# The first mixer's three output projections: from fp32 products to split products in the heads' three weight slots

## The reference, cut to what matters

```
y_a = o.reshape(b, s, V_W) @ w_gdn_proj              # o: the eight heads' outputs, normed and gated
y_b = (gb * causal_depthwise_conv(gc * xin, sc_conv_w)) @ w_sc_out
mix = (gate_a * y_a + gate_b * y_b) @ w_o
```

## Time and profile before

| what | value |
|---|---|
| median of 3 runs | 1449.14 us (1444.05, 1449.14, 1450.11) |
| profiled execution, its own time | 1441.25 us |
| its span, first to last instruction | 1439.5 us |
| mean granted TensorE clock | 0.977 |
| PE, DVE, ACT busy | 94%, 62%, 45% of the span |
| L742, all three projections | 256 + 128 records, busy 58.8 + 28.0 us |
| DMA | 188 GB/s mean |

### The profile page before, as it was taken

How to read it: one execution, slowest core, us unless ns; L and a number is a source line. 1 busy time by engine, 2 the same in 40 slices (tenths; PEclk the granted TensorE clock), 3 DMA queues, 4 the chain that set the end, 5 groups by cost and what they waited for, 6 DMA issues and landing times.

```text
span 1439.5 us, 26382 instructions
## 1 busy us (share of the span) xinstructions
PE 1355.4 (94%) x9801; PEld 1236.9 (86%) x9801; DVE 894.9 (62%) x1680; ACT 643.2 (45%) x1171; POOL 14.9 (1%) x82
## 2 busy tenths in 40 slices
PE   6999999999999899999799987999999999999997
PEld 3888889988888799999578876999996777899996
DVE  0677887877623477778555635787785432775553
ACT  2555554555331355444555424555443331544542
POOL 4000000000000000000000000000000000000000
PEclk9999999999999899999899999999999999899998
DMA  9655545655692189889568812898896272666562
GB/s 310 194 162 162 175 121 159 178 159 161 177 248 59 33 245 268 265 245 317 147 207 255 228 44 77 252 271 263 242 317 226 76 195 70 178 203 185 158 182 88
DMA packets 400018, 269.95 MB, mean 188 GB/s; under 512 B 9915, under 2 KB 357425, under 8 KB 399937
## 3 DMA queue, kind: packets, MB, share of 16 engines
q1 hardware_dynamic: 399936, 268.83, 63.4%
HBM read 267.75 MB, written 1.05 MB: 187 GB/s over the span
## 4 chain that ended last, share of the span: by engine, by line
PE 83%; DVE 8%; ACT 3%; issue 2%; SPq 2%; DMA 1%; DVEq 0%; ACTq 0%
PE bank L756 18%; PE bank L758 18%; PE bank L757 18%; PE bank L742 6%; PE bank L818 4%; PE bank L728 2%; DVE w_low L1828 2%; PE bank L1150 1%; PE bank L952 1%; PE bank L953 1%; PE bank L944 1%; PE bank L1179 1%; DVE h_parts L1844 1%; SPq L527 1%; ACT w_high L1343 1%
## 5 line engine op out<-in xcount | busy, mean ns | idle before, releaser
L756 PE MATMUL bank<-h_parts,w_high 128*128 128x256 f32 x1824 | 547.9, 300 | 18.2 <-DVE h_parts L1844 15.7
L757 PE MATMUL bank<-h_parts,w_high 128*128 128x256 f32 x1824 | 520.2, 285 | 0.0
L758 PE MATMUL bank<-h_parts,w_low 128*128 128x256 f32 x1824 | 520.0, 285 | 0.0
L1828 DVE TENSOR_TENSOR w_low<-w_raw,w_high 128x1024 fp32r<-128x1024 f32 (+2 forms) x324 | 361.6, 1124 | 100.1 <-ACT w_high L1343 88.6
L756 PEld LDWEIGHTS bank<-h_parts,w_high 128*128 128x128 f32 x1824 | 352.8, 193 | 40.2 <-issue 24.9
L757 PEld LDWEIGHTS bank<-h_parts,w_high 128*128 128x128 f32 x1824 | 354.4, 194 | 2.9 <-issue 2.6
L758 PEld LDWEIGHTS bank<-h_parts,w_low 128*128 128x128 f32 x1824 | 353.5, 194 | 0.0
L1343 ACT ACTIVATE w_high<-w_raw 128x1024 fp32r<-128x1024 f32 (+2 forms) x324 | 312.9, 973 | 64.9 <-DMA w_raw<-in_w_ffn_out 19.5
L756 PE MATMUL bank<-act_parts,w_high 128*128 128x256 f32 x528 | 148.7, 282 | 0.0
L1335 ACT ACTIVATE evac<-bank 128x256 f32<-128x256 f32 x140 | 53.6, 383 | 212.1 <-PE bank L758 188.1
L757 PE MATMUL bank<-act_parts,w_high 128*128 128x256 f32 x528 | 147.3, 279 | 0.0
(11 more groups left out here) (360 smaller groups left out, 1576.4 us busy)
## 6 DMA issues: line engine op xcount, KB each, us to landing
ada_w<-in_ada_w SPq DMA_DIRECT2D x48, 1024.0 KB, 6.2
w_raw<-in_ffn_w_in SPq DMA_DIRECT2D x88, 512.0 KB, 4.1
w_raw<-in_w_in SPq DMA_DIRECT2D x72, 512.0 KB, 3.9
w_raw<-in_w_ffn_in SPq DMA_DIRECT2D x44, 512.0 KB, 4.0
ada_w<-in_w_ada SPq DMA_DIRECT2D x16, 1024.0 KB, 7.6
w_raw<-in_gla_w_in SPq DMA_DIRECT2D x24, 512.0 KB, 6.1
w_raw<-in_ffn_w_out SPq DMA_DIRECT2D x32, 384.0 KB, 4.8
w_raw<-in_ffn_w_out SPq DMA_DIRECT2D x32, 320.0 KB, 3.4
```

What stands on the lines that cost most here:

```text
L756: pe.matmul(acc[:, 0:T], hi[:, n, :], x_parts[:, k, 0, :], start=k == 0, stop=False)
L757: pe.matmul(acc[:, 0:T], hi[:, n, :], x_parts[:, k, 1, :], start=False, stop=False)
L758: mm = pe.matmul(acc[:, 0:T], lo[:, n, :], x_parts[:, k, 0, :], start=False, stop=k == kb - 1)
L1828: dve.tensor_tensor(w_low[:, s, 0:m], w_raw[:, s, 0:m], w_high[:, s, 0:m].bitcast(F32), ALU.subtract)\
```

## The change

The three projections become split products of one stream `st_p` of 24 pieces, which follows the heads' 72 in the same three slots: `w_sc_out` 0 to 7, `w_gdn_proj` 8 to 15 (`PA`), `w_o` 16 to 23 (`O1`). Their operands get halves as well:
- `ybin` becomes `y_high` and `y_low`. In `short_conv` DVE's one multiply becomes three instructions: the product rounded, the product again in fp32, and the difference. This stands in every head.
- For `w_gdn_proj` the parts go to `h1_parts`: in the eighth recurrence one ACT copy of seven blocks (128 x 1792) for the high halves, two DVE subtractions (four and three blocks) for the low ones, and two small DVE instructions for the last block.
- For `w_o` each block of `hT` gets `mix_high` on ACT and `mix_low` on DVE, in `h_parts`.

DVE and ACT make the weights' halves at the places where the heads' are made. In the eighth recurrence these are `low1(2)` to `low1(8)` and pieces 9 and 10; afterwards piece j+3 follows block j.

```diff
...
     pieces = 0
+    last_piece = {}
...
         SplitStream.pieces += n * per
+        self.raw_free = [SplitStream.last_piece.get(s, 0) for s in range(slots)]
...
-        oall, ybin = big[:, 0:KB, :], big[:, KB:2 * KB, :]
+        oall = big[:, 0:KB, :]
+        y_high = h_parts[:, KB // 2:KB, :, :].rearrange("p k a t -> p (k a) t")
+        y_low = ring_rest[:, 0:KB * T].rearrange("p (k t) -> p k t", t=T)
...
         st_h1 = SplitStream(H1, 9, slots=3)
-        for at in H1_SLOTS:
-            Stream.slot_user[at] = st_h1.end
-        st_pb = Stream(1, KB, [3, 7, 11, 0, 1, 2, 4, 5])
-        st_pa = Stream(1, KB, [6, 8, 9, 10, 3, 0, 1, 2])
-        st_o1 = Stream(1, KB, [12, 13, 14, 15, 16, 17, 7, 11])
+        st_p = SplitStream(1, 3 * KB, slots=3)
+        PA, O1 = KB, 2 * KB
+        for at in range(SplitStream.RINGS, 2 * HALF):
+            Stream.slot_user[at] = st_p.end
...
                 for j in range(st.per):
-                    if j >= st.slots or follows:
+                    if st is st_f1 and j < st.slots:
+                        if st.raw_free[j]:
+                            sp.wait_ge(S("split"), st.raw_free[j])
+                    elif j >= st.slots or follows:
...
             wo = kview(a["w_o"][0])
-            load_all(st_pb, wb)
-            load_all(st_pa, wa, range(4))
-            load_all(st_o1, wo, range(6))
-            load_ada(A_FFN1)
-            load_all(st_pa, wa, range(4, KB))
-            load_all(st_o1, wo, range(6, KB))
+            def ada2(i, j):
+                if j == PA + 2:
+                    load_ada(A_FFN1)
+            split_stream(st_p, lambda i, j: (wb, wa, wo)[j // KB][:, :, j % KB * P:(j % KB + 1) * P], IN_PARTS, extra=ada2, follows=True)
...
+                x_high, x_low = x_parts if isinstance(x_parts, tuple) else (x_parts[:, :, 0, :], x_parts[:, :, 1, :])
...
                                           ready=None if chain or j else ("h_low", 0))
-                        elif j < st_pb.per:
-                            pe.wait_ge(S("short"), 5 * H1)
-                            block_product(st_pb, 0, j, bank[j % 3], ybin, 3, part=[k])
+                        elif j < KB:
+                            if k == 0:
+                                pe.wait_ge(S("short"), 7 * H1)
+                                pe.wait_ge(S("evacuated"), st_p.done(0, j) + 3 - 3)
+                            split_product(st_p, 0, j, bank[j % 3], (y_high, y_low), IN_PARTS[0], KB, part=[k])
...
             head1(H1, False, True)
-            pe.wait_ge(S("evacuated"), st_pa.block0 + 3)
+            pe.wait_ge(S("evacuated"), st_p.done(0, PA - 1) + 3)
+            pe.wait_ge(S("part_low"), 2)
             for j in range(2):
-                block_product(st_pa, 0, j, bank[j], oall, 2, part=range(H1 - 1))
+                split_product(st_p, 0, PA + j, bank[j], h1_parts, IN_PARTS[0], KB, part=range(H1 - 1))
             pe.wait_ge(S("mod_ready"), 3)
-            pe.wait_ge(S("head_out"), H1)
+            pe.wait_ge(S("part_low"), 3)
             for j in range(KB):
-                block_product(st_pa, 0, j, bank[j % 2], oall, 2, part=[H1 - 1] if j < 2 else None)
+                pe.wait_ge(S("evacuated"), st_p.done(0, PA + j) + 3 - 2)
+                split_product(st_p, 0, PA + j, bank[j % 2], h1_parts, IN_PARTS[0], KB, part=[H1 - 1] if j < 2 else None)
...
                     norm_sum(1, range(KB - 2))
-                block_product(st_o1, 0, j, bank[j % 2], hT, 2, ready=("mix_ready", 0))
+                pe.wait_ge(S("evacuated"), st_p.done(0, O1 + j) + 3 - 2)
+                split_product(st_p, 0, O1 + j, bank[j % 2], h_parts, IN_PARTS[0], KB, ready=("part_low", 3) if j == 0 else None)
...
                     high(st_h1, i + 1, j - 6, IN_PARTS)
+                else:
+                    high(st_p, 0, j - 6, IN_PARTS)
...
                             copy_out1(i, j, last)
-                        elif j < st_pb.per:
-                            copy_out(st_pb, 0, j, hT[:, j, :], 3)
+                        elif j < KB:
+                            copy_out(st_p, 0, j, hT[:, j, :], 3)
+                            high(st_p, 0, j + 3, IN_PARTS)
...
                     copies(4 + 2 * l)
+                    if not gemm and l == 2:
+                        act.wait_ge(S("gemm_done"), st_h1.end)
+                        act.wait_ge(S("head_out"), H1 - 1)
+                        act.activation(h1_parts[:, 0:H1 - 1, 0, :], oall[:, 0:H1 - 1, :], ACT.Copy).then_inc(S("part_high"), 1)
...
+            def mix_high(j):
+                act.wait_ge(S("mix_ready"), j + 1)
+                act.activation(h_parts[:, j, 0, :], hT[:, j, :], ACT.Copy).then_inc(S("part_high"), 1)
...
                 act.wait_ge(S("mixed"), j + 1)
-                copy_out(st_pa, 0, j, evac[:, j % 2, :], 2)
-            out_blocks(st_o1, "o_added", 0, 4, 2)
+                copy_out(st_p, 0, PA + j, evac[:, j % 2, :], 2)
+                if j:
+                    mix_high(j - 1)
+                high(st_p, 0, PA + j + 3, IN_PARTS)
+            mix_high(KB - 1)
+            for j in range(KB):
+                act.wait_ge(S("o_added"), j + 1)
+                copy_out(st_p, 0, O1 + j, evac[:, j % 4, :], 2, scale=mod[:, 2 * KB + j:2 * KB + j + 1])
+                if O1 + j + 3 < st_p.per:
+                    high(st_p, 0, O1 + j + 3, IN_PARTS)
...
-                dve.wait_ge(S("short"), 5 * n + TAPS2 + 1)
-                dve.tensor_tensor(part(ybin, i), scv, scb, ALU.mult).then_inc(S("short"), 1)
+                dve.wait_ge(S("short"), 7 * n + TAPS2 + 1)
+                dve.tensor_tensor(part(y_high, i), scv, scb, ALU.mult).then_inc(S("short"), 1)
+                dve.tensor_tensor(scv, scv, scb, ALU.mult).then_inc(S("short"), 1)
+                dve.wait_ge(S("short"), 7 * n + TAPS2 + 3)
+                dve.tensor_tensor(part(y_low, i), scv, part(y_high, i).bitcast(F32), ALU.subtract).then_inc(S("short"), 1)
...
+                def low1(j):
+                    if gemm:
+                        low(st_h1, i, j, IN_PARTS)
+                    else:
+                        low(st_p, 0, j, IN_PARTS)
...
                     dve.tensor_scalar(gmat[:, NT + t, :], ident[:, :], hcur[:, 2 + t:3 + t], None, ALU.mult).then_inc(S("gmat"), 1)
-                if gemm:
-                    low(st_h1, i, 2, IN_PARTS)
+                low1(2)
...
 ...
...
                         convolve(i, l - 1)
-                    if gemm:
-                        if l < LEVELS - 1:
-                            low(st_h1, i, l + 4, IN_PARTS)
-                        elif not last:
-                            low(st_h1, i + 1, 0, IN_PARTS)
+                    if l < LEVELS - 1:
+                        low1(l + 4)
+                    elif gemm and not last:
+                        low(st_h1, i + 1, 0, IN_PARTS)
+                    else:
+                        low(st_p, 0, 0 if gemm else 9, IN_PARTS)
+                    if not gemm and l in (3, 4):
+                        at = slice(0, 4) if l == 3 else slice(4, H1 - 1)
+                        dve.wait_ge(S("part_high"), 1)
+                        dve.tensor_tensor(h1_parts[:, at, 1, :], oall[:, at, :], h1_parts[:, at, 0, :].bitcast(F32), ALU.subtract)\
+                           .then_inc(S("part_low"), 1)
...
                     short_conv(i)
-                    if not last:
-                        low(st_h1, i + 1, 1, IN_PARTS)
+                if gemm and not last:
+                    low(st_h1, i + 1, 1, IN_PARTS)
+                else:
+                    low(st_p, 0, 1 if gemm else 10, IN_PARTS)
...
                 dve.wait_ge(S("silu"), 2 * n)
+                if not gemm:
+                    dve.tensor_tensor(h1_parts[:, c, 0, :], part(oall, c), onrm, ALU.mult).then_inc(S("part_high"), 1)
                 dve.tensor_tensor(part(oall, c), part(oall, c), onrm, ALU.mult).then_inc(S("head_out"), 1)
+                if not gemm:
+                    dve.wait_ge(S("part_high"), 2)
+                    dve.wait_ge(S("head_out"), H1)
+                    dve.tensor_tensor(h1_parts[:, c, 1, :], part(oall, c), h1_parts[:, c, 0, :].bitcast(F32), ALU.subtract)\
+                       .then_inc(S("part_low"), 1)
...
             dve.wait_ge(S("gates"), 2)
-            dve.wait_ge(S("evacuated"), st_pb.end + 3)
+            dve.wait_ge(S("evacuated"), st_p.done(0, PA - 1) + 3)
...
             dve.wait_ge(S("gated"), 1)
+            def mix_low(j):
+                dve.wait_ge(S("part_high"), 2 + j + 1)
+                dve.tensor_tensor(h_parts[:, j, 1, :], hT[:, j, :], h_parts[:, j, 0, :].bitcast(F32), ALU.subtract).then_inc(S("part_low"), 1)
             for j in range(KB):
-                dve.wait_ge(S("evacuated"), st_pa.done(0, j) + 3)
+                dve.wait_ge(S("evacuated"), st_p.done(0, PA + j) + 3)
...
                 dve.sem_inc(S("mixed"), 1)
+                if j:
+                    mix_low(j - 1)
```

(36 more changed lines are left out.)

22 lines of the change are left out of this document (9 added, 13 removed).

## The result

| | before | after |
|---|---|---|
| median of 9 runs each | 1449.14 us | 1439.28 us |
| lowest to highest | 1444.05 to 1451.58 | 1435.62 to 1444.85 |
| profiled execution, its own time and span | 1441.25, 1439.5 us | 1440.99, 1439.3 us |
| its mean granted clock | 0.977 | 0.971 |

The medians of these runs lie 9.9 us apart. Forecast were 8.1 less and 1441.0. Yet the two profiled executions have the same time. That of before, 1441.25 us, was faster than all 55 timed runs of that kernel here (1442.8 and more), at a clock near the top of the 0.966 to 0.978 of the 46 whose clock is on record. So the two traces are compared part by part, and a part in which the clock fell is not compared by its length alone.

The account below looks back on a forecast made before the run. PE, busy for 94% of the span, was taken as the bound: -14.3 us for its products, +5.1 for short_conv, +1.1 where w_o begins, -8.1 in sum, from 1449.1 to 1441.0 us; range 1433 to 1448 us.

Parts of the forecast that it names:

- PE's gain of 14.3 us: Three projections, 192 steps: split products for fp32 ones save 9.8 us outside the eighth recurrence and 4.5 inside.
- The step of 0.357 in the blocks: Blocks of w_gdn_proj and w_o: a step takes 0.357 us instead of 0.434, 9.8 us less over 128 steps.
- The 0.07 for a step in the eighth recurrence: Eighth recurrence: each of 64 steps gets 0.07 us shorter, 4.5 us in all.
- Rival 2: Projections: three passes cost three quarters of four, so PE gains 20.9 us; net -14.7, 1434.4 us; chance 6%.
- short_conv, 5.1 us: Added DVE instructions delay PE: 0.93 us in heads 2, 4, 6, 0.5 in 3, 5, 7, 0.8 at eighth recurrence.
- The halves in the eighth recurrence, the last head's output, the blocks: 0: Eighth recurrence through the blocks of w_gdn_proj: the new ACT and DVE work is covered and costs 0.
- The start of w_o, 1.1 us: First block of w_o: PE idles 1.1 us at step 7 for the last low half; bounds 0 and 2.3.
- Rival 4: The three weight slots become the bound, from a load of 6.3 us on; net +9.0, 1458 us; chance 7%.
- Rival 3: Odd heads +1.3, w_o start +1.2, eighth recurrence's ACT copy and subtractions +2.4; net -3.2, 1445.9 us; 25% with Rival 5.
- Rival 5: PE's clock falls once for some 8 us around the new idles: +4, net -4.1, 1445.0 us; 25% with Rival 3.

Follow-up runs that it names:

- Experiment 1: The kernel before, unchanged, run once more for a second trace: 1446.15 us, ratio 0.9994; its profiled execution took 1455.08 us.
- experiment 2: The kernel before with only short_conv's second multiply and subtraction added, their result not used: 1451.98 us, ratio 1.0036 to the kernel before.
- experiment 7: The changed kernel without the projections' third product except at each block's last step, so part of the result is missing: 1433.15 us, ratio 0.9898.
- Experiment 3: The changed kernel with short_conv's second multiply and subtraction moved later, ahead of the kk_done wait or behind gmat: 1434.32 us, ratio 0.9918.
- experiment 4: The changed kernel with the halves of hT's block 7 made ahead of those of weight piece 18: 1436.99 us, ratio 0.9934.
- 5: The changed kernel with the edits of Experiment 3 and experiment 4 together: 1433.99 us, ratio 0.9911 to the kernel before.
- experiment 6: As 5, with the low half of the next head's weight piece 1 moved behind gmat: 1434.21 us, ratio 0.9907.

## Why the prediction was right

The stretch from the first product to the norm, and what the clock took in it, in five executions (us):

| kernel | first product to norm | clock took | without it |
|---|---|---|---|
| before | 106.87 | 0 | 106.9 |
| before, again | 110.21 | 3.4 | 106.8 |
| 2, additions alone | 108.57 | 1.7 | 106.9 |
| after | 98.58 | 5.1 | 93.5 |
| two products | 88.23 | 8.5 | 79.7 |

The longer stretch, from the first L983 to the norm, in all nine (us):

| kernel | first L983 to norm | clock took | without it |
|---|---|---|---|
| before | 368.3 | 0 | 368.3 |
| before, again | 371.8 | 3.4 | 368.4 |
| 2, additions alone | 374.8 | 1.7 | 373.1 |
| after | 365.6 | 5.1 | 360.5 |
| 3 | 358.0 | 3.4 | 354.6 |
| 4 | 361.8 | 1.7 | 360.1 |
| 5 | 355.6 | 1.7 | 353.9 |
| 6 | 358.3 | 3.4 | 354.9 |
| 7, two products | 355.2 | 8.5 | 346.7 |

- **PE's gain of 14.3 us.** Confirmed as a sum: the stretch is 13.4 us shorter without the clock, and -14.3 + 1.1 = -13.2 was forecast for it. The step of 0.357 in the blocks measured 0.358. The 0.07 for a step in the eighth recurrence is confirmed too: the level that the earlier trace rows show at 3.93 us takes 3.51 here, at full clock.

```profile
414.47 0.60 PE L940 MATMUL bank<-scratch 128*128 128x128 f32 x4
...
417.98 0.60 PE L940 MATMUL bank<-scratch 128*128 128x128 f32 x4
```

  Rival 2 (-20.9) is refuted. The rule of the Trainium skill's "FP8 and Floating Point Precision" (TensorE Precision Notes) for fp32 may hold for the passes, but in this kernel the three products did not take three quarters of the fp32 step: 0.358 of 0.434 is 0.82.
- **short_conv, 5.1 us.** The first product came 5.60 us later. By the heads: even ones +0.92, +0.91 and +0.94 (0.93 forecast), odd ones +0.70, +0.66 and +0.74 (0.5 forecast), the eighth's start +0.70 (0.8 forecast). The mis-sized term is that of the odd heads, and it has two parts. The first is the price of a wait: the rows show 0.39 us of idle in head 5 and 0.17 in head 7, beside the 0.37 worked out, but behind L919 these heads are 0.66 and 0.44 late. The prediction gave a reason for the difference, and it is so in the rows of before: the weights of L923 load at 343.87 us in head 7, 0.12 ahead of the matmul, and in head 6, where it waits, at 300.19 together with it. It took 0.13 for this, and it is 0.27. The second part is not `short_conv`'s and stands nowhere in the prediction: ACT and DVE make the halves of the new stream's first pieces in head 7, where before no weight was left to prepare. The other 0.30 us of head 7's 0.74 arise at the end of its round, 0.20 at L976 and 0.10 at L983; ACT's copy for L983 stands behind one of these halves:

```profile
385.28 1.05 ACT L1342 ACTIVATE w_high<-w_raw 128x1024 fp32r<-128x1024 f32 x1
386.23 0.38 ACT L1495 ACTIVATE scratch<-bank 128x256 f32<-128x256 f32 x1
```

  Experiment 3, with no wait at L921 in head 7, keeps these 0.30 (43.51 against 43.21), and experiment 2, which has no such halves, has +0.35 in all. In the eighth's start the second multiply began 0.35 and the difference 0.80 us after the first multiply, as worked out. The Trainium skill's "The DRAIN you can't avoid" ("VectorE: DVE Perf Modes") has the next instruction begin when the one ahead has emptied the pipe, but adds that one which is not held starts earlier; the prediction took up the first half alone. The rows have the second multiply begin 0.35 us after an instruction of 0.43 did, which agrees with the addition.
- **The halves in the eighth recurrence, the last head's output, the blocks: 0.** From 388.74 us to the norm PE waited for no weight's half, and for no half of an activation before `w_o`. What this term left out is head 7, as said above: 0.30 us. DVE's round measured 2.50 us (2.6 forecast).
- **The start of w_o, 1.1 us.** 0.85 measured, at step 7 and on the last low half as said; experiment 4 takes it away.
- **Rival 4**, the three slots: refuted; no PE wait on a load, and the loads of the three weights landed in 4.0 to 4.1 us (median), where 6.3 was the point from which it decides.
- **Rival 3**, more joints: only the odd heads, +0.6 us of its 4.9, and half of that from the halves in head 7, which it did not name.
- **Rival 5**, the clock: in the profiled execution it happened, twice, and took about 5 us. With 3.3 us more behind the norm, where the change touches nothing, the clock took 8.4 us more than in the first execution of before, so that the two profiled executions come out alike (-7.8 + 8.4). Experiment 1 shows that before had the same falls and that its first profiled execution was the one without. Of nine profiled executions seven have a fall between 424 and 440 us, all but the first of before and experiment 4. At the eighth's first product (386 to 396 us) it fell in three of the four executions with a wait of 1.38 us or more (after, 4 and 7; not 2), and in one of the five with a shorter wait (before, again). Whether the longer wait makes that fall likelier is open: so few executions don't tell it.

The sum: -13.4 + 5.6 = -7.8 us from the traces, -8.1 forecast, -7.4 (by the interval, -5.1 to -9.7) from the runs.

## What to carry to other kernels

Where one engine is busy for 94%, count the work taken from it with the spacing of the same instructions elsewhere in the trace, then look for every place where it already waits for the engine that gets new work: each addition there is paid once for each round, in full where the engine already waits (0.9 us in the even heads) and in good part where the slack is small (0.4 to 0.7 in the odd), here over 5 of 13.4 us gained. Count also the round in which the new work starts, where before there was none of its kind (head 7). A result that only some later step needs belongs behind the instructions for which the bound engine waits (experiments 3 and 4 together, that is 5, give 5.5 us back by the ratios); but a wait may only move, as in experiment 6, so compare the round's length and not the wait. Profile the kernel before more than once when a change is worth under 1%: a single execution can be the exception.

## What the runs showed of the hardware

- The time follows the granted clock from run to run: over the 95 runs of the eight kernels here whose clock is on record, 0.001 of mean clock goes with 0.85 us (one slope fitted within the kernels). The runs of before alone span 0.966 to 0.978 and some 12 us.
- At both ends of the eighth recurrence, where PE waits 0.5 to 1.5 us at a time, the clock falls to 0.50 (1.2 GHz) in one execution and not in the next of the same code. Split steps then start every 0.64 us instead of 0.36 (L750 at 434.32 and 434.96 us in after).
- Taking work from PE gave only about half back in experiment 7 (7.4 us by the ratios, 13.8 by the trace without the clock). In its runs the mean clock was lower (0.966 to 0.970, after 0.972 on average). That the new gaps brought it down was not shown.
- Where a matmul that did not wait begins to, the idle that its row shows is less than the cost: at L919 heads 5 and 7 show 0.39 and 0.17 us and are 0.66 and 0.44 late behind it, 0.27 more both times; in head 7 of experiment 2 the row has no idle that the profile would print, and it is 0.34 late. In the even heads, which waited before, idle and cost grew alike (0.90 and 0.92). In experiment 6 the idle row is gone, and the even round is as long as before.
